# Hybrid decoder step on one core: bias loads moved to SyncE, sample rows stacked, ten idle products on TensorE

## What is computed

```
p = h @ w_in                                   # 1024 -> all the projections
o_a, S_a = hgrn2(q_a, f_a, i_a)                # mixer A, recurrent state per head
o_b, S_b = gated_delta(conv(qkv_b), beta, g)   # mixer B, recurrent state per head
merged = sigmoid(gate_a) * (ya @ w_oa) + sigmoid(gate_b) * (yb @ w_ob)
x = x + merged @ w_out
logits = rmsnorm(x) @ w_router + b_router
top_val, top_idx = top_k(logits, 4); gates = softmax(top_val)
for each expert e, on the rows that chose it:
    gu = rows @ w_gu[e] + b_gu[e]              # 1024 -> 2048
    hmid = (clip(up) + 1) * min(gate, 7) * sigmoid(1.702 * gate)
    y   += gates * (hmid @ w_down[e] + b_down[e])
out = rmsnorm(x + y)
```

## Time and profile before

| | |
|---|---|
| median of 3 runs | 1301.12 us (1301.07 to 1301.78) |
| the profiled execution's own time | 1299.87 us |
| its span, first to last instruction | 1298.1 us |
| PE busy | 1255.6 us, 97% |
| DVE, ACT, POOL busy | 509.9, 241.4, 70.5 us |
| moved by DMA | 450.76 MB, mean 347 GB/s |
| mean granted clock of PE | 0.989 |
| first expert product / last expert product | 353.75 us / about 1284.7 us |

### The profile page before, as it was taken

The page is one execution under the profiler, slowest core; times in us unless marked ns, Lnnn a source line. Parts: engine busy times, 40 slices in busy tenths (PEclk is TensorE's granted clock), DMA queues, the critical chain, the costliest instruction groups (busy, mean ns, idle before and its releaser), DMA issues.

```text
span 1298.1 us, 19089 instructions
## 1 busy us (share of the span) xinstructions
PE 1255.6 (97%) x7395; PEld 545.0 (42%) x7395; DVE 509.9 (39%) x1058; ACT 241.4 (19%) x411; POOL 70.5 (5%) x157
## 2 busy tenths in 40 slices
PE   7999989989999999999999999999999999999996
PEld 5887757665533333333333333333333333333331
DVE  2184884354444332332233332332233332332245
ACT  3124422233411111111111111111111111111103
POOL 3002102000300000000000000000000000000001
PEclk9999999899799999999999999999999999999999
DMA  9454208529499999999999999999999999999990
GB/s 310 140 173 140 80 26 268 152 83 421 153 377 422 429 429 429 429 428 428 428 429 428 429 428 428 428 429 429 428 428 428 428 429 428 430 428 429 416 411 35
DMA packets 60934, 450.76 MB, mean 347 GB/s; under 512 B 9242, under 2 KB 18576, under 8 KB 35960
## 3 DMA queue, kind: packets, MB, share of 16 engines
q1 hardware_dynamic: 55764, 446.20, 83.4%
q10 hardware_dynamic: 5132, 4.03, 1.1%
HBM read 444.05 MB, written 6.26 MB: 347 GB/s over the span
## 4 chain that ended last, share of the span: by engine, by line
PE 60%; DVE 7%; issue 4%; DVEq 0%; ACT 0%; ACTq 0%
PE ps L1099 34%; PE ps L1129 12%; PE ps L1033 6%; PE ps L1061 4%; DVE x_tok L1922 3%; PE ps L1078 2%; DVE proj L1896 2%; DVE proj L1890 2%; PE ps L1086 1%; PE ps L1048 1%; PE ps L1051 1%; DVE x_tok L1989 0%; DVE feat L1895 0%; DVE proj L1899 0%; DVE proj L1889 0%
## 5 line engine op out<-in xcount | busy, mean ns | idle before, releaser
L1099 PE MATMUL ps<-ring,feat 128*64 128x512 f32 x1568 | 358.7, 600 | 0.0
L1129 PE MATMUL ps<-ring,proj 128*64 128x512 f32 x992 | 237.7, 601 | 0.0
L1099 PEld LDWEIGHTS ps<-ring,feat 128*64 128x64 f32 x1568 | 105.6, 137 | 185.3 <-issue 177.8
L1922 DVE TENSOR_TENSOR x_tok<-x_tok,ps 128x512 f32<-128x512 f32 (+1 forms) x192 | 122.6, 679 | 78.2 <-PE ps L1061 75.4
L1889 DVE TENSOR_SCALAR proj<-ps 128x512 f32<-128x512 f32 x32 | 22.1, 691 | 304.3 <-PE ps L1099 303.4
L1129 PEld LDWEIGHTS ps<-ring,proj 128*64 128x64 f32 x992 | 63.0, 136 | 112.9 <-issue 110.4
L1413 ACT ACTIVATE proj<-ps,wide 128x512 f32<-128x512 f32 x32 | 22.0, 688 | 441.0 <-DVE wide L1904 430.8
L673 PE MATMUL ps<-feat,ring 128*128 128x264 f32 x384 | 93.8, 397 | 0.0
L640 PE MATMUL ps<-feat,ring 128*128 128x280 f32 (+1 forms) x384 | 90.5, 398 | 0.4 <-DVEq L1483 0.4
L1033 PE MATMUL ps<-proj 128*64 128x512 bf16 x558 | 83.7, 391 | 0.0
L640 PEld LDWEIGHTS ps<-feat,ring 128*128 128x128 f32 x384 | 72.7, 190 | 17.4 <-issue 0.5
(11 more groups left out here) (384 smaller groups left out, 1091.9 us busy)
## 6 DMA issues: line engine op xcount, KB each, us to landing
ring<-in_w_gu SPq DMA_DIRECT2D x96, 2048.0 KB, 19.6
ring<-in_w_down SPq DMA_DIRECT2D x62, 2048.0 KB, 18.0
states<-in_w_gu SPq DMA_DIRECT2D x15, 2048.0 KB, 19.0
proj<-in_w_gu SPq DMA_DIRECT2D x15, 2048.0 KB, 19.8
ring<-in_w_in SPq DMA_DIRECT2D x11, 2048.0 KB, 8.8
ring<-in_w_gu SPq DMA_DIRECT2D x4, 1024.0 KB, 7.9
ring<-in_w_in SPq DMA_DIRECT2D x2, 1024.0 KB, 9.0
out<-states SPq DMA_DIRECT2D x1, 2048.0 KB, 8.7
```

The source lines that it names most:

```text
L1099: last = mm(bank(j // 2)[64 * (j % 2):64 * (j % 2) + 64, :], xgT[:, k % 4, k // 4, :], w[:, 512 * j:512 * j + 512], start=False, stop=k == ...
L1129: last = mm(bank(y)[64 * j:64 * j + 64, :], h[:, k % 4, 64 * (k // 4):64 * (k // 4) + 64], w[:, n:n + 512], start=False, stop=k == KT - 1)
L1922: tt(x, x, bank(banks[i][j])[0:r, :], ALU.add).then_inc(sg["comb_taken"], 1)
```

## The change

- **Bias loads.** The six loads of `b_gu` and `b_down` and that of `b_router` leave ACT's program; SP issues them, the six behind the store of the first prompt state, the seventh behind the store of the second.
- **Sample parts stacked.** The three bfloat16 parts of the 8 sample rows lie below each other in one tile, `smp_parts`: part 0 from row 0, part 1 from row 32, part 2 from row 64, zeros between. Their ranks are copied to the same rows, so one product over 128 rows does what three did. `pick_rows` issues 14 products in place of 18. `turn_share` uses all 128 rows of the third tile in place of 8.
- **The first expert's rows.** Of the full tiles only tile 0 is split ahead of the first expert, and its rests are computed by DVE (`rest_of_first` and a row behind `take_xT(1)`), not by POOL. The samples go in as one float32 product per half (`hot_smp`), and their splitting moves behind the first expert's fetch.
- **DVE.** `selb` is computed in `select`, behind the signal `sel_made`, no longer in `place`.
- **Idle products.** `keep_warm(n)` issues n products of `ident_bf` with `x2_parts[0]`, 128x128 by 128x512 bfloat16, into PSUM bank 3, whose content nobody reads then: 2 ahead of `turn_x2(1, 1)`, 3 in the middle of `logits(2)`, 2 behind the counts, 3 ahead of `turn_rows(0)`.

```diff
+            sp.wait_ge(sg["oA_done"], NCH)
+            sp.wait_ge(sg["silu_done"], 2)
+            for p in range(3):
+                sp.dma_start(b_f32[NE * p:NE * p + NE, 0:2 * D], b_gu[0]).then_inc(sg["bias_in"], 16)
+                sp.dma_start(b_f32[NE * p:NE * p + NE, 2 * D:3 * D], b_down[0]).then_inc(sg["bias_in"], 16)
...
+            sp.dma_start(br_b, b_router.to_broadcast([128, NE])).then_inc(sg["route_in"], 16)
...
+            def keep_warm(n):
+                pe.wait_ge(sg["x2_high"], 1)
+                for _ in range(n):
+                    mm(bank(3), ident_bf, x2_parts[0][:, 0, 0:512], start=True, stop=True)
...
+            keep_warm(2)
             turn_x2(1, 1)
-            logits(2)
+            logits(2, 0, 4)
+            keep_warm(3)
+            logits(2, 4, KT)
             pe.wait_ge(sg["hot_built"], 1)
             for q, name in enumerate(("x2_high", "x2_mid", "x2_low")):
-                pe.wait_ge(sg[name], 2)
...
+                pe.wait_ge(sg[name], 1)
+                for j in range(2):
+                    mm(bank(2)[64 * j:64 * j + 64, :], hot[:, 0, :], x2_parts[0][:, q, 512 * j:512 * j + 512],
+                       start=q == 0, stop=False)
+            for j in range(2):
+                mm(bank(2)[64 * j:64 * j + 64, :], hot_smp, x2h[0:NS, 2, 512 * j:512 * j + 512], start=False, stop=False)
             count_ranks(2)
...
             last.then_inc(sg["cnt_done"], 1)
+            keep_warm(2)
...
-                    for i in range(NI):
+                    for i in range(2):
                         for j in range(2):
...
+                for j in range(2):
+                    last = mm(bank(2)[64 * j:64 * j + 64, :], hot[:, 2, :], smp_parts[:, 512 * j:512 * j + 512],
+                              start=False, stop=True)
                 last.then_inc(sg["rows_picked"], 1)
...
             last.then_inc(sg["rows_picked"], 1)
+            keep_warm(3)
             turn_rows(0)
...
-            for p in range(3):
-                act.dma_start(b_f32[NE * p:NE * p + NE, 0:2 * D], b_gu[0]).then_inc(sg["bias_in"], 16)
-                act.dma_start(b_f32[NE * p:NE * p + NE, 2 * D:3 * D], b_down[0]).then_inc(sg["bias_in"], 16)
...
-            act.dma_start(br_b, b_router.to_broadcast([128, NE])).then_inc(sg["route_in"], 16)
...
             add_mix(1, 0)
+            rest_of_first()
             take_xT(1)
+            dve.wait_ge(sg["x2_mid"], 1)
+            L.tell(tt(x2_parts[0][:, 2, :], x2h[:, 0, :], x2_parts[0][:, 1, :], ALU.subtract), "x2_low", 1)
             select(1)
```

More of the change, by code:

```diff
@@ L571, in _ @@
             gp.sem_inc(sg["route_consts"], 1)
+            L.tell(gp.memset(projf[:, 10368:10880], 0.0), "parts_zero")
             def pick(out, b, name):
                 gp.tensor_copy(out, eh3[:, bass.ds(b, 1)].to_broadcast([3 * NE, CAP])).then_inc(sg[name], 1)
[L576 to L586, removed]
+            pick(sel_gu, 0, "sel_gu_ready")
+            pool.wait_ge(sg["rows_picked"], 1)
+            pool.wait_ge(sg["x2_high"], 2)
+            L.tell(gp.tensor_tensor(x2h[0:NS, 2, :], x2h[0:NS, 2, :], smp_parts[0:NS, :], ALU.subtract), "x2_rest", 2)
+            pool.wait_ge(sg["x2_high"], 3)
+            L.tell(gp.tensor_tensor(x2h[:, 1, :], x2h[:, 1, :], x2_parts[1][:, 0, :], ALU.subtract), "x2_rest", 3)
+            pool.wait_ge(sg["x2_mid"], 2)
+            L.tell(gp.tensor_tensor(smp_parts[2 * C:2 * C + NS, :], x2h[0:NS, 2, :], smp_mid, ALU.subtract), "x2_low", 2)
+            pool.wait_ge(sg["x2_mid"], 3)
+            L.tell(gp.tensor_tensor(x2_parts[1][:, 2, :], x2h[:, 1, :], x2_parts[1][:, 1, :], ALU.subtract), "x2_low", 3)
             pick(sel_dn, 0, "sel_dn_ready")
@@ L1367, in normed, with high, middle, high_samples @@
                 L.tell(f(x2h[0:r, i, :], x_tok[0:r, i, :], ACT.Copy, scale=rstd[0:r, i:i + 1]), "x2_normed", p + 1)
[L1369 to L1378, removed]
+            def high(i, n):
+                L.tell(f(x2_parts[i][:, 0, :], x2h[:, i, :], ACT.Copy), "x2_high", n)
+            def middle(i, n):
+                act.wait_ge(sg["x2_rest"], n)
+                L.tell(f(x2_parts[i][:, 1, :], x2h[:, i, :], ACT.Copy), "x2_mid", n)
+            def high_samples():
+                act.wait_ge(sg["parts_zero"], 1)
+                L.tell(f(smp_parts[0:NS, :], x2h[0:NS, 2, :], ACT.Copy), "x2_high", 2)
+            def middle_samples():
+                act.wait_ge(sg["x2_rest"], 2)
+                L(f(smp_mid, x2h[0:NS, 2, :], ACT.Copy))
+                L.tell(f(smp_parts[C:C + NS, :], smp_mid, ACT.Copy), "x2_mid", 2)
             square_sum(0)
@@ L1424, in _ @@
             act.wait_ge(sg["lg_done"], NI)
-            high(2)
-            middle(2)
+            high_samples()
+            high(1, 3)
+            middle_samples()
+            middle(1, 3)
             take_rows(1)
@@ L1819, in select, with rest_of_first @@
                 L.tell(v.tensor_reduce(selm[0:r, i, :], oneh[0:r].rearrange("p j e -> p e j"), AX.X, ALU.add), "sel_made", p + 1)
+                L(ts(selb[0:r, i], selm[0:r, i], FAR, -FAR, ALU.mult, ALU.add))
+            def rest_of_first():
+                dve.wait_ge(sg["x2_high"], 1)
+                L.tell(tt(x2h[:, 0, :], x2h[:, 0, :], x2_parts[0][:, 0, :], ALU.subtract), "x2_rest", 1)
             def place(p):
@@ L1823, in place @@
                 r = ROWS[i]
-                L(ts(selb[0:r, i], selm[0:r, i], FAR, -FAR, ALU.mult, ALU.add))
                 dve.wait_ge(sg["rank_done"], max(p + 1, 2))
                 L(tt(rank[0:r, i, 0:NE], bank(7)[0:r, NE * i:NE * i + NE], selb[0:r, i], ALU.add))
[L1827 to L1830, removed]
+                out = (hot_smp, hot[:, 0, :], hot_f32)[p]
+                ins = tt(out, iota_s[0:r, 0:CAP], rank[0:r, i, 0:1].to_broadcast([r, CAP]), ALU.is_equal)
                 if p:
@@ L1876, in _ @@
             tt(xgT, turned, w_norm, ALU.mult).then_inc(sg["xg_ready"], 1)
+            for q in range(1, 3):
+                L(v.tensor_copy(rank[C * q:C * q + NS, 2, 0:NE], rank[0:NS, 2, 0:NE]))
             dve.wait_ge(sg["rows_picked"], 1)
```

30 lines of the change are left out of this document (12 added, 18 removed).

## The result

The changed kernel takes 1281.77 us (median of four runs, 1278.06 to 1285.33) against 1301.45 us for the kernel before on the same chip: a ratio of 0.9848 [0.9813, 0.9883]. Forecast were 1285.4 us and a range from 1282.5. The sign was right; the size was 3.6 us short, and the median lies just outside the range. The profiled execution took 1279.04 us, with a span of 1277.3; for it the forecast was 1284.2, 5.2 us too much.

What follows compares the result with a forecast made beforehand. The prediction took the experts' weight queue (29.37 us an expert) as the bound, barely slower than PE. Savings of 2.7 + 2.6 + 7.0 + 3.4 = 15.7 us gave a median of 1285.4 us, range 1282.5 to 1294.5.

Steps and rivals of the forecast that it cites:

- What bounds the kernel: In the experts, the weight queue at 29.37 us an expert was already slower than PE at 29.19, hidden by PE's head start.
- a lead of 7.2 us: PE's head start over the weight queue at pass 2, predicted used up after about ten experts at 0.74 us each.
- Bias loads and the clock behind them: At mixer B's first link: 2.7 us of PE idle time saved, plus 2.6 us because PE's clock no longer falls.
- Routing: From the third tile's logits to the first expert: shorter work and full clock, less idle products, save 7.0 us.
- The first rival: The clock falls in the routing despite the idle products, leaving 7.1 us saved in all: 1294.0 us; chance 0.14.
- The stacked samples: In each expert's pick, two of nine product pairs go, 0.56 us an expert; 3.4 us in all, not 17.4.
- `turn_share` with 128 rows in place of 8 loads and streams the same columns: nothing: In the experts, using 128 rows instead of 8 in `turn_share` was claimed to change the time by nothing.
- The queue runs without a gap: The weight queue was claimed full from first issue at 357.43 to 1267.8 us, 910 us, its length unchanged.
- The last two picks: At the stream's end, where loads have more room, two picks were to save 2 x 0.56 us.
- The ends that I named for the terms: Low and high values for the savings across the whole kernel, said to give 12.3 to 17.5 us off.
- queue is no limit: In the experts, transfers run faster if asked sooner, so each expert keeps 0.56 us: 1271.4 us; chance 0.04.
- the queue's pace suffers: In the experts, more loads waiting slow the 910 us stream, 9.1 us per cent; 1306 us at 2.3%; chance 0.03.

Runs made afterwards that it cites:

- the second profile of the changed kernel: Profile from rerunning the changed kernel unaltered; that rerun's median was 1280.69 us, the profiled execution 1281.75 us.
- The third execution of the changed kernel: Profile from running the changed kernel unaltered a third time; that run's median was 1282.1 us, ratio 0.9857 to the kernel before.

## Why the prediction was right and where it failed

*What bounds the kernel:* right. PE was ahead of a queue that needs 29.37 us an expert, by a lead of a few us, and with a shorter pass it waits at the fifth step of the expert, right behind the turning of the hidden rows:

```profile
531.14 0.75 PE L1097 MATMUL ps<-ident,proj 128*128 128x128 f32 x4
532.80 1.51 PE L1118 MATMUL ps<-ring,feat 128*64 128x512 f32 x6 [0.91 <-DMA ring<-in_w_gu]
```

This is the first such wait, in about the seventh expert where I said the twelfth, for 1.5 us a pass where I said 0.7. Both follow from the one wrong number below: a lead of 7.2 us lasts 4.4 passes at 29.37 - 27.75 = 1.62 us each.

*Bias loads and the clock behind them,* 2.7 + 2.6: right in the changed kernel's profile (5.4 by the links), and right by the same links in both single tests (5.3 with the loads taken off ACT, 5.3 with them put back). The medians of these tests bracket it, 3.4 us from one side and 7.1 from the other; that the difference is the clock's later falls is shown for the two profiles and only likely for the other runs.

*Routing,* 7.0: in the profile 12.63 - 5.4 = 7.2, right. But that this one profile hits it so closely is partly luck, for it is a run in which the clock did not fall. It fell there in one of the three profiles of the changed kernel and in six of the seven of its variants. The first rival, which I had priced at 8.6 us with a chance of 0.14, therefore came true in part, at a fraction of its price: 1.3 us for the 3.4 us at half clock that the second profile of the changed kernel shows.

*The stacked samples, "two of nine pairs go: 2 x 0.28 = 0.56 us an expert":* **this is the step that failed.** It is 1.44 us. Dividing 2.53 by 9 spread the cost of the 8-row products over all. A pair of 128 rows costs 0.215 and a group of two such pairs and an 8-row pair 0.86, so the cheap part of the mean was what stayed. And "`turn_share` with 128 rows in place of 8 loads and streams the same columns: nothing" failed in the same way, by 0.27. The weight-load rows of the trace had shown it.

*"The queue runs without a gap":* the second failure. In its first 40 us it moved 15.55 MB before and 15.99 now, in its last 60 us 23.9 and 24.7: 1.2 MB at 428 GB/s are the 2.9 us of the table. At both ends few loads are under way: in the kernel before, a load issued at 378.18 us landed 10.5 us later, one issued at 1212.75 landed 11.0 later, and between them the delay of a pass's third load was 18.5 to 23.1. SP issues a load when PE has read its buffer, so PE's pace sets the queue's there; that this is the reason is argued from these delays, and no run tests it alone. The last two picks gave 2 x 1.44 and the lead 2.3, together 5.2, as measured in this profile (6.7 and 5.3 in the two others). At my own pass of 28.63 us the table of passes gives by interpolation between 28.92 and 28.18 some 936.1, a gain of 4.6 us instead of 3.4: so by this estimate 1.2 of the 4.8 us missed in the experts is this term and 3.6 the mis-sized pass.

*The range.* The ends that I named for the terms add up to at most 2.8 + 2.9 + 7.8 + 3.4 = 16.9 us, not 17.5, and the stacked samples had no ends at all: the range was narrow just where the miss lay. That the median is off by only 3.6 us and the profiled execution by 5.2 is chance too. I had put the median 1.25 above that execution, and it lay 2.7 above.

*The rivals "queue is no limit" and "the queue's pace suffers":* both out. The pass ends at 29.36 us, though the last load took 24.0 us to land, and not 19.5.

## What to carry to other kernels

Don't price the products that go by the mean of a mixed group: look at the weight loads between them, and price each form by itself. A queue that is full in the middle may still follow the engine at its first and its last buffers; read GB/s at the two ends before calling a saving hidden. And where the clock of one program differs from run to run, take ten times and several profiles before crediting one us to an edit.

## What the hardware showed that was not expected

**Weight loads with fewer rows.** A 128-row load behind 128-row products is hidden (0.215 us a pair), an 8-row load behind them is not, nor a 128-row load behind it: 0.2 us more each time the rows change and change back. The Trainium skill, TensorE: Matmul & The Clock Gate, The mechanism (in Part 3), says that weight loads overlap with running products only when the row group differs, though its text also names a background weight buffer as a way to load ahead; here loads on the same 128 rows overlap, and an 8-row load among them and the 128-row load behind it don't, and the measurement decides. Its section LDWEIGHTS says that a load's time goes by its columns and not its rows; the rows agree (0.10 and 0.12 us), but the time in which nothing else runs is what counts.

**The clock falls in one run and not in the next, behind the same work.** PE in two executions of the changed kernel, first that with 1279.04 us:

```profile
192.79 0.42 PE L795 MATMUL ps<-ring 32*32 32x128 f32 x8 [1.42 <-DVE ring L1687]
...
194.09 3.73 PE L682 MATMUL ps<-feat,ring 128*128 128x264 f32 x16
```

and that with 1281.75:

```profile
192.76 0.42 PE L795 MATMUL ps<-ring 32*32 32x128 f32 x8 [1.42 <-DVE ring L1687]
...
194.17 5.29 PE L682 MATMUL ps<-feat,ring 128*128 128x264 f32 x16
```

The same sixteen products take 1.56 us more: the granted clock is at half, 1.2 GHz, from about 194 to 197 us, behind the same idle time of 1.42 us and the same products. The mean clock of a run goes with its time, roughly: 0.998 in the runs of 1278 to 1279.4 us, 0.992 to 0.995 in those of 1284.5 to 1285.4. What decides it stays open. Idle products, ten, twenty or placed otherwise, left 0 to 6.8 us at half in the routing, against 13.6 to 17.1 without them.

**A slower start without a lower granted clock.** The third execution of the changed kernel above (1281.08 us in its profile) had no stretch below 1.00 ahead of its last 5 us, like the first, and yet its stream began 2.4 us later. It lost them in the first group of products:

```profile
13.91 13.82 PE L649 MATMUL ps<-feat,ring 128*128 128x280 f32 x48 [0.18 <-DVEq L1504]
```

against, in the execution of 1279.04 us:

```profile
13.82 11.56 PE L649 MATMUL ps<-feat,ring 128*128 128x280 f32 x48 [0.35 <-DVEq L1504]
```

The same 48 products took 11.56 us in nine of the profiles and 13.3 to 13.9 in four, among them the one without idle products and the kernel before with them. It comes long before anything the change touches, and adds up to 2 us of chance to every comparison of single profiles.
